# One core's hybrid attention and PEER layer: a quarter of the U subtraction on VectorE, picks in PSUM, a first input block in halves

## The reference, cut to what matters

```python
def _peer(h, w_q, subkeys, u_tab, v_tab):              # h: 256 tokens x 2048
    q = (xt @ w_q).reshape(t, PEER_HEADS, 2, PEER_QDIM // 2)
    scores = jnp.einsum('thpd,hpkd->thpk', q, subkeys)
    vals, idx = lax.top_k(scores, PEER_TOPK)           # 16 of 128, twice a head
    cand_s = (vals[:, :, 0, :, None] + vals[:, :, 1, None, :]).reshape(t, PEER_HEADS, -1)
    top_s, sel = lax.top_k(cand_s, PEER_TOPK)          # 16 of 256 pairs
    ...
        act = jax.nn.gelu(jnp.einsum('tkd,td->tk', u_tab[eb], xb), approximate=False)
        return jnp.einsum('tk,tkd->td', gb * act, v_tab[eb])

def reference(x, w_in, ...):
    for l in range(DEPTH):                             # DEPTH = 1
        mix = _hybrid_mixer(h, ...)                    # projections, GLA and retention heads, w_out
        h = _layer_norm(DEEPNORM_ALPHA * h + mix, ln1_g[l], ln1_b[l])
        ffn = _peer(h, w_peer_q[l], peer_subkeys[l], peer_u[l], peer_v[l])
        h = _layer_norm(DEEPNORM_ALPHA * h + ffn, ln2_g[l], ln2_b[l])
```

## Time and profile before

| | |
|---|---|
| median of 3 runs | 2074.11 us (2072.78 to 2075.37) |
| the profiled execution | 2073.22 us |
| its span | 2071.4 us |
| TensorE busy | 2031.9 us, 98% |
| VectorE busy | 1231.7 us, 59% |
| GpSimd busy | 1103.5 us, 53% |
| ScalarE busy | 968.9 us, 47% |
| DMA | 381.29 MB, mean 184 GB/s |

### The profile page before, as it was taken

How to read it: one execution, slowest core, us unless ns; L and a number is a source line. 1 busy time by engine, 2 the same in 40 slices (tenths; PEclk the granted TensorE clock), 3 DMA queues, 4 the chain that set the end, 5 groups by cost and what they waited for, 6 DMA issues and landing times.

```text
span 2071.4 us, 34214 instructions
## 1 busy us (share of the span) xinstructions
PE 2031.9 (98%) x11230; PEld 1765.9 (85%) x11230; DVE 1231.7 (59%) x2137; ACT 968.9 (47%) x1435; POOL 1103.5 (53%) x697
## 2 busy tenths in 40 slices
PE   8999999989999999999999999999999999999997
PEld 8998888879988888888888888888888888888885
DVE  1744111123978777658999999965555555555557
ACT  4544334434445556584444444444444444444442
POOL 6877778886778899998777777710000000000000
PEclk9999999999999999999999999999999999999998
DMA  8655657576667777786666666665555555555553
GB/s 269 173 153 170 194 168 253 181 202 174 161 157 180 175 172 185 190 191 166 163 162 162 162 162 162 163 261 195 189 198 187 199 187 201 185 200 185 200 185 139
DMA packets 148994, 381.29 MB, mean 184 GB/s; under 512 B 15536, under 2 KB 17712, under 8 KB 131136
## 3 DMA queue, kind: packets, MB, share of 16 engines
q1 hardware_dynamic: 148928, 380.40, 64.0%
HBM read 376.15 MB, written 4.19 MB: 184 GB/s over the span
## 4 chain that ended last, share of the span: by engine, by line
PE 81%; POOL 6%; issue 5%; DVE 3%; DMA 3%; DVEq 1%; ACT 1%; SPq 1%; POOLq 0%; ACTq 0%
PE ps L1406 33%; PE ps L1366 15%; PE ps L1367 8%; PE ps L1144 7%; PE ps L1146 6%; PE ps L1145 6%; POOL u_lo L1117 4%; PE ps L1348 3%; POOL w_lo L1085 3%; DMA u_raw<-in_peer_u 2%; DVE u_t L831 1%; PE ps L1236 1%; DMA raw<-in_w_in 1%; SPq L335 0%; PE ps L1140 0%
## 5 line engine op out<-in xcount | busy, mean ns | idle before, releaser
L1366 PE MATMUL ps<-xT,u_hi 128*128 128x512 f32 x2048 | 726.9, 399 | 7.5 <-POOL u_lo L1117 7.1
L1117 POOL TENSOR_TENSOR u_lo<-u_t,u_hi 128x512 fp32r<-128x512 f32 x512 | 667.9, 1327 | 123.0 <-ACT u_hi L510 121.1
L1367 PE MATMUL ps<-xT,u_lo 128*128 128x256 f32 x2048 | 571.8, 279 | 0.0
L1085 POOL TENSOR_TENSOR w_lo<-raw,w_hi 128x1024 fp32r<-128x1024 f32 x176 | 430.1, 2452 | 127.8 <-ACT w_hi L387 127.5
L510 ACT ACTIVATE u_hi<-u_t 128x512 fp32r<-128x512 f32 x512 | 319.9, 632 | 370.3 <-DVE u_t L831 369.9
L1366 PEld LDWEIGHTS ps<-xT,u_hi 128*128 128x128 f32 x2048 | 384.3, 188 | 100.5 <-POOL u_lo L1117 13.2
L831 DVE STREAM_TRANSPOSE u_t<-u_raw 128x512 f32<-128x512 f32 x512 | 351.6, 699 | 106.0 <-DMA u_raw<-in_peer_u 78.8
L1367 PEld LDWEIGHTS ps<-xT,u_lo 128*128 128x128 f32 x2048 | 386.2, 189 | 0.0
L1090 POOL TENSOR_TENSOR small<-small 128x1 f32<-128x1 f32 (+1 forms) x3 | 2.2, 745 | 708.0 <-DVE small L1045 707.9
L387 ACT ACTIVATE w_hi<-raw 128x1024 fp32r<-128x1024 f32 x176 | 186.0, 1059 | 287.0 <-PE ps L1146 273.8
L1406 PE MATMUL ps<-v_hi,m_lo 128*128 128x512 f32 x1024 | 316.5, 389 | 0.0
(11 more groups left out here) (182 smaller groups left out, 2319.2 us busy)
## 6 DMA issues: line engine op xcount, KB each, us to landing
u_raw<-in_peer_u SPq DMA_DIRECT2D x512, 256.0 KB, 4.7
v_raw<-in_peer_v SPq DMA_DIRECT2D x128, 1024.0 KB, 4.8
raw<-in_w_in SPq DMA_DIRECT2D x112, 512.0 KB, 3.8
raw<-in_w_out SPq DMA_DIRECT2D x32, 512.0 KB, 3.8
raw<-in_w_peer_q SPq DMA_DIRECT2D x128, 128.0 KB, 3.8
x_sb<-in_x SPq DMA_DIRECT2D x4, 512.0 KB, 9.3
x_again<-in_x SPq DMA_DIRECT2D x1, 2048.0 KB, 8.6
h_dram<-o_sb SPq DMA_DIRECT2D x1, 2048.0 KB, 8.3
```

The source lines that it names most:

```text
L1085: pool.tensor_tensor(w_lo[:, k, :], raw[:, k, :], w_hi[:, k % HI_RING, :].bitcast(F32), ALU.subtract).then_inc(lo_done, 1)
L1117: pool.tensor_tensor(u_lo[:, r, :], u_t[:, r, :], u_hi[:, r, :].bitcast(F32), ALU.subtract).then_inc(ulo_done, 1)
L1366: pe.matmul(acc, u_hi[:, r, c], xT[:, :, kt, :], start=kt == 0, stop=False)
L1367: ins = pe.matmul(acc[:, 0:T], u_lo[:, r, c], xT_hi[:, kt, :], start=False, stop=kt == KT - 1)
```

## The change

Three things are changed.

1. In tiles 0 to 63 the low part of a tile's fourth quarter is made by VectorE, in a new function `u_late`. It stands in VectorE's program behind the second transpose of the next tile. GpSimd makes three quarters of these tiles. TensorE waits for the fourth quarter on a semaphore of its own, `ulo_late`. From tile 64 on GpSimd makes all four.
2. `pick` is a tensor of 128 x 1024 in two PSUM banks instead of SBUF. There is room for one part only, so the stages 0, 1, 2 of a part follow each other in three tiles. The row of numbers of stage 0 is read from `iota_ps`, which ScalarE now fills after tile 5 instead of at tile 52.
3. The first weight step and the first block of x come in two halves each. The queue begins with 256 columns of x; the constants `keepc` are issued by ScalarE. The first of the turned pieces waits for the first half of x only. The first weight step is copied and subtracted in halves of 512 columns, and TensorE's first half step waits for the first.

```diff
-        pick = at("pick", BIG + 64 * K, [P, TT * PH * TOPK, TOPK])
+        pick = bank(2, 2).rearrange("p (n a) -> p n a", a=TOPK)
...
-            sp.dma_start(keepc[:], keep_c).then_inc(keep_in, 16)
-            for b in range(4):
-                c = slice(b * COL, (b + 1) * COL)
+            x_cols = lambda c0, n: (x_sb[:, :, c0:c0 + n], x[0].rearrange("(a p) d -> p a d", p=P)[:, :, c0:c0 + n])
+            sp.dma_start(*x_cols(0, COL // 2)).then_inc(x_half, 16)
+            sp.dma_start(raw[:, 0, 0:COL], win[0:P, GQ:GQ + COL]).then_inc(raw_half, 16)
+            sp.dma_start(raw[:, 0, COL:2 * COL], win[P:2 * P, GQ:GQ + COL]).then_inc(raw_in[0], 16)
+            sp.dma_start(*x_cols(COL // 2, COL // 2)).then_inc(x_in[0], 16)
+            load_step(0, 1, win, GQ)
+            for b in range(1, 4):
...
-            for c in range(2):
-                hi_steps(0, (c,))
-                act_turn(act, 0, c)
+            act.dma_start(keepc[:], keep_c).then_inc(keep_in, 16)
+            act.wait_ge(raw_half, 16)
+            act.activation(w_hi[:, 0, 0:COL], raw[:, 0, 0:COL], ACT.Copy).then_inc(hi_half, 1)
+            act.wait_ge(raw_in[0], 16)
+            act.activation(w_hi[:, 0, COL:2 * COL], raw[:, 0, COL:2 * COL], ACT.Copy).then_inc(hi_done, 1)
+            act_turn(act, 0, 0)
+            hi_steps(0, (1,))
+            act_turn(act, 0, 1)
...
             for j in range(2, 6):
                 u_tile(0, j)
+            act.wait_ge(score_sb, 4)
+            act.activation(iota_ps, iota, ACT.Copy).then_inc(iota_done, 1)
...
-                p4 = pick[:, rows].rearrange("p (h k) a -> p h k a", h=4)
+                p4 = pick.rearrange("p (h k) a -> p h k a", h=4)
...
+            def u_late(ii, j):
+
+                r = slot(j, 3)
+                dve.wait_ge(uhi_done, ii * 24 + 4 * j + 4)
+                dve.tensor_tensor(u_lo[:, r, :], u_t[:, r, :], u_hi[:, r, :].bitcast(F32), ALU.subtract).then_inc(ulo_late, 1)
...
             for i in range(U_TURN // 6 * 6):
                 for f in range(4):
                     u_quarter(i // 6, i % 6, f)
+                    if i and f == 1:
+                        u_late(i // 6, i % 6 - 1)
...
                     elif U_PICK <= i and f == 1:
                         n = i - U_PICK
-                        route_pick(n // 12, n // 6 % 2, n // 2 % 3, n % 2)
+                        route_pick(n // 12, n // 6 % 2, n % 3, n // 3 % 2)
...
-            with pool.Fori(0, P // 6) as ii:
+            with pool.Fori(0, U_SPREAD // 6) as ii:
+                for n in range(24):
+                    if n % 4 < 3:
+                        u_low(ii, n)
...
-                    pe.wait_ge(ulo_done, ii * 24 + 4 * j + f + 1)
+                    if spreads:
+                        pe.wait_ge(ulo_done, ii * 24 + 4 * j + f + 1 - U_SPREAD)
+                    elif f < 3:
+                        pe.wait_ge(ulo_done, ii * 18 + 3 * j + f + 1)
+                    else:
+                        pe.wait_ge(ulo_late, ii * 6 + j + 1)
```

More of the change, by code:

```diff
@@ L897, in route_pick @@
                 else:
-                    dve.tensor_reduce(ijg[:, s, a, h0 * TOPK:(h0 + 4) * TOPK], pick[:, rows], AX.X, ALU.add).then_inc(ijg_done, 1)
+                    dve.tensor_reduce(ijg[:, s, a, h0 * TOPK:(h0 + 4) * TOPK], pick, AX.X, ALU.add).then_inc(ijg_done, 1)
             def route_gates():
@@ L939, in _ @@
                         u_quarter(ii, j, f)
+                        if f == 1:
+                            u_late(ii, j - 1)
                         if f == 2:
@@ L982, in u_spread_tile @@
                 u_quarter(ii, j, 1)
+                if isinstance(q, int) and q == 0:
+                    u_late(ii, j - 1)
                 if weighs:
@@ L1095, in head_power @@
                 pool.tensor_tensor(half(rstd), half(var16), half(power), ALU.pow).then_inc(rstd_done, 1)
-            with pool.Fori(0, V_END) as g:
+            pool.wait_ge(hi_half, 1)
+            pool.tensor_tensor(w_lo[:, 0, 0:COL], raw[:, 0, 0:COL], w_hi[:, 0, 0:COL].bitcast(F32), ALU.subtract).then_inc(lo_half, 1)
+            pool.wait_ge(hi_done, 1)
+            pool.tensor_tensor(w_lo[:, 0, COL:2 * COL], raw[:, 0, COL:2 * COL], w_hi[:, 0, COL:2 * COL].bitcast(F32), ALU.subtract).then_inc(lo_done, 1)
+            lo_steps(0, range(1, STEPS))
+            with pool.Fori(1, V_END) as g:
                 lo_steps(g, range(STEPS))
@@ L1117, in u_low @@
                 pool.tensor_tensor(u_lo[:, r, :], u_t[:, r, :], u_hi[:, r, :].bitcast(F32), ALU.subtract).then_inc(ulo_done, 1)
-            with pool.Fori(0, P // 6) as ii:
+            with pool.Fori(0, U_SPREAD // 6) as ii:
+                for n in range(24):
+                    if n % 4 < 3:
+                        u_low(ii, n)
+            for n in range(24):
+                if n % 4 < 3 or n >= 4 * (U_SPREAD % 6):
+                    u_low(U_SPREAD // 6, n)
+            with pool.Fori(U_SPREAD // 6 + 1, P // 6) as ii:
                 for n in range(24):
@@ L1159, in steps_n @@
                         acc_wait(g)
-                    pe.wait_ge(lo_done, STEPS * g + k + 1)
+                    if g == 0 and k == 0:
+                        pe.wait_ge(lo_half, 1)
+                    else:
+                        pe.wait_ge(lo_done, STEPS * g + k + 1)
                     for kt in (2 * k, 2 * k + 1):
+                        if g == 0 and kt == 1:
+                            pe.wait_ge(lo_done, 1)
                         for n in range(4):
@@ L1194, in _ @@
             pe.wait_ge(keep_in, 16)
-            turned_group(0, steps_n, x_sb, 0, lambda c: (x_in[c // 2], 16), lead=2)
+            turned_group(0, steps_n, x_sb, 0, lambda c: (x_in[c // 2] if c else x_half, 16), lead=2)
             pe.wait_ge(glrw_lo, 1)
```

21 lines of the change are left out of this document (12 added, 9 removed).

## The result

The changed kernel takes 2078.67 us (median of 13 runs), the kernel before 2073.91 (13 runs): ratio 1.0022 [1.0014, 1.003]. It is slower by 4.8 us, where 5.0 were forecast. One run of 4304.16 us is left out of the ratio; it counts in the median, which is 2078.6 without it. The profiled execution took 2076.4 us, 2.3 less than its kernel's median, with a span of 2074.6.

The account below looks back on a forecast made before the run. The prediction took the two-buffer load loop as the U stage's bound: 3.4 + 3.5 - 0.6 = +6.3, less 1.3 for the start, +5.0 us, so 2078.2 against 2073.22 (2079.1 beside the median); range 2067.5 to 2084.

Parts of the forecast that it names:

- What bounds the kernel: U stage: tiles wait for loads into two buffers, not for GpSimd; the load loop explains 5.80 of 5.85 us a tile.
- T = (L + D)/2: U tiles that wait for their load: time per tile is half of L plus D; 5.80 us in tiles 25 to 48.
- L: U tile loads: time from a buffer's release to the next tile's landing in it, about 7.15 us.
- D: VectorE in a U tile: start of first to end of fourth transpose, mean 4.44 us in tiles 25 to 48.
- third rival: U tile loads get quicker: L falls by 0.6, the addition costs nothing, only the start shows; 2072.8 us, chance 0.08.
- first rival: U stage: GpSimd is the bound, so tiles 25 to 48 run at 5.65 each; 2067.9 us, faster, chance 0.17.
- The fourth quarter on VectorE: Tiles 0 to 63: one subtraction of four leaves GpSimd and adds 0.61 us to VectorE, inside D.
- the race with GpSimd: Each U tile: VectorE's new subtraction starts before GpSimd's first quarter, by 0.2 us, and delays that quarter by 0.5 us.
- The picks in PSUM: Tiles 25 to 47: picks no longer exclude GpSimd, take 1.23 us; D of tile 32 falls from 5.06 to 4.19.
- The two stretches: Tiles 3 to 24 lose 3.5 us (bounds 2.5 and 5.1), tiles 25 to 48 lose 3.4 (3.0 to 3.6).
- Tiles 49 to 63: Pace by load 5.4 us, under TensorE's 5.56: no cost, and 0.6 us taken off.
- The start: First weight step and x block: first product near 8.7 us, 1.5 earlier, worth 1.3 us (bounds 0.5 and 2.2).

Follow-up runs that it names:

- dose outside: Kernel before plus one unneeded VectorE multiply (128x512, PSUM) behind the fourth transpose in each of tiles 25 to 47: 2073.79 us, ratio 1.0001.
- dose inside: Kernel before plus one unneeded VectorE multiply (128x512, PSUM) behind the second transpose in each of tiles 25 to 47: 2081.84 us, ratio 1.0039.
- subtraction outside D: Changed kernel with VectorE's subtraction moved behind the tile's own fourth transpose, after the buffer is released: 2082.64 us, ratio 1.0044 to the kernel before.
- the four buffers: Changed kernel with four load buffers instead of two for U tiles 8 to 47: 2062.32 us, ratio 0.9944 to the kernel before.
- unheld: Not the held run, where TensorE's first four transposes also wait for x's second half (new start, PSUM picks, four buffers, GpSimd subtracting all): 2064.29 us.
- start, picks, four buffers: Changed kernel with four load buffers and all four quarters subtracted by GpSimd again: 2059.38 us, ratio 0.9931; run again 2061.67 us, 0.994.

## Why the prediction was right

**What bounds the kernel.** Right. The rule T = (L + D)/2 was read from two tiles and holds over all of them where the first transpose waits for its load: averages over tiles 25 to 47 (L to the landing itself, waited for or not), with TensorE's pace as the last column:

| kernel | L | D | (L + D)/2 | pace |
|---|---|---|---|---|
| before | 7.19 | 4.54 | 5.86 | 5.87 |
| changed | 7.23 | 4.80 | 6.02 | 6.05 |
| start and picks only | 7.29 | 4.23 | 5.76 | 5.78 |
| dose outside | 7.21 | 4.46 | 5.84 | 5.89 |
| dose inside | 7.22 | 5.14 | 6.18 | 6.30 |
| subtraction outside D | 7.20 | 4.19 | 5.69 | 5.90 |

In the last two VectorE comes late to landed loads more often, by 0.39 and 0.62 us on average (0.19 to 0.29 in the others), and the rule gives only a floor. The mean of D before is 4.54 and not the 4.44 of the prediction, so the rule gives 5.86 and not 5.80, beside a measured pace of 5.87. L stayed fixed, which disposes of the third rival (quicker loads); the four buffers took the loop away and TensorE's own pace came out, 5.57 and 5.65 a tile. The first rival (GpSimd is the bound) would have had tiles 25 to 48 under 140 us; they took 145.09.

**The fourth quarter on VectorE.** 0.65 us each, 642 to 654 ns in all 64, so the race with GpSimd is won every time, as worked out; the margin of 0.2 us was enough. GpSimd's first quarter pays 0.28 us for it, where 0.5 was said. D rose by 0.58 (4.16 to 4.74), 0.61 was said. The experiment outside D shows what stood behind that margin.

**The picks in PSUM.** 1.23 as said, D 4.16 against the 4.19 worked out for tile 32. Their own worth is 3.2 us by time and 1.9 in tiles 25 to 48.

**The two stretches.** Tiles 3 to 24: +1.8 against +3.5; tiles 25 to 48: +4.6 against +3.4; together 6.4 against 6.9. The sizes of both parts were off, for one reason at their border. Up to the first product of tile 24 (713.12 - 587.69 = 125.43 after) the loss is 3.5, as walked: before it was 712.29 - 590.34 = 121.95, by this row of before:

```profile
712.29 0.39 PE L1366 MATMUL ps<-xT,u_hi 128*128 128x512 f32 x1
```

Between tiles 24 and 25 TensorE waited 2.40 us before and 0.59 after, and 1.7 us comes back. At tile 25 the first compare stretched GpSimd's first quarter to 2.29; now it takes 1.58. I had put the relief of that stretch into D alone, and so into the later tiles. The run with the picks alone bears this out: from tile 24's first product to tile 25's it takes 6.72 us, the kernel before 8.12, the changed one 6.43. In the later tiles the loss is larger for it, because TensorE enters them without a tile's slack; that last clause is argued, not shown.

**Tiles 49 to 63.** -0.2 against -0.6.

**The start.** The pair of profiles shows 571.80 - 569.16 = 2.6 us, twice what was said and over my bound of 2.2; the average over twelve profiles is 1.3, what was said. Before was a late execution of its kind (the others with the old start are at 569.6 to 570.9), and after an early one. The mechanism held: first product 8.40, 8.7 was said. The rise moved more than the 1.5 us I allowed, from 16.2 to 10.9 by the granted clock. Part of it is luck: with the old start it came at 12.9, 12.9, 13.6, 15.2 and 16.2, with the new one (unheld) between 10.7 and 12.4.

**Sum.** +5.0 forecast, +4.8 by the medians, +3.2 between the two profiled executions. By parts, timed: start alone -2.0, picks alone -3.2, subtraction +7.6, sum +2.4; each has an interval of about 2 us to either side, so they agree with 4.8 only within it. Start and picks together, in the kernel against which the subtraction is priced, give -2.9, and -2.9 + 7.6 is the +4.7 of the whole.

That the forecast came within 0.2 us is in part luck. Taken apart, it had the subtraction at +10.2 (24 tiles of half 0.61, which is 7.3, and 3.5, and -0.6), the picks at -3.9 (the 3.4 forecast for tiles 25 to 48 less that 7.3) and the start at -1.3. The subtraction cost 7.6, and start and picks gave 2.9 where 5.2 stood in the sum: two terms that were each about 2.5 us too large, of opposite sign, at the edge of what these intervals can tell. The profiles say the same of the first: the subtraction costs 6.3 us in tiles 25 to 48 (145.09 against 138.80), and 2.6 in tiles 3 to 24 (131.85 against 129.25) where 3.5 was walked. The mechanism is shown; the nearness of the total is not its merit alone.

## What to carry to other kernels

With two buffers and a fixed time L from release to landing, what counts on the engine that empties them is the time from its first to its last read of a buffer. An instruction put between these reads costs about half its length per tile, even on an engine that idles, as long as tiles wait for their loads; behind the last read it is free if the engine has idle time there, nothing that it needs is late and no other engine holds its port. Before moving work off the engine that looks full, ask which wait comes last; here 16 KB of each partition for two more buffers was worth 16 us to the changed kernel (2078.67 to 2062.32), and the moved quarter nothing.

## What had not been expected of the hardware

TensorE's pace in stretches where it never stands is not the same in each execution. Busy in tiles 49 and on, the same kernel twice (start, picks, four buffers):

```profile
860.00:930.00 70.00, 70.00 (x408) 61.28 (x407) 39.17 (x63) 51.73 (x91) 62.34 (x51) 1.00 0.78 189
```

and in its second execution:

```profile
860.00:930.00 70.00, 70.00 (x400) 60.82 (x399) 38.33 (x62) 51.07 (x90) 61.80 (x49) 1.00 0.76 185
```

Busy all the time at full clock, and 408 products against 400; tiles 49 to 63 took 84.08 and 85.45 us. Over the thirteen profiles this stretch is at 83.9 to 84.2 or at 85.4 to 85.9. Tile by tile it is one of two paces: a tile takes 5.55 or 5.65 us, tens of tiles in a row. In the first of the two executions tiles 24 to 49 go at 5.65 and tiles 52 to 63 at 5.55, with the turning of the picks between them; in the second both go at 5.65. With four buffers and the moved quarter nearly all go at 5.55. So most of the 2.0 us between 133.67 and 135.68 in tiles 25 to 48 is a step that the same kernel takes or doesn't take, and no gain of VectorE's subtraction can be read from it. What decides it stays open. It alone is 1.4 us, half of what the smaller parts of this change are worth, so a stage table of one pair of profiles can't settle them.

TensorE's rise to 2.4 GHz at the start came anywhere from 10.7 to 16.4 us by the granted clock in thirteen executions, and 2.3 us apart in two whose first work and first products started at the same time: at 12.9 us with a first transpose at 7.26 and a first product at 9.76 (picks alone), and at 15.2 with 7.27 and 9.77 (dose outside).
